# A conformer layer on 8 cores: attention outputs in any two of four PSUM banks, scaled by a stream of their own; tables loaded ahead, the gate by Tanh, the conv's square sums on TensorE

## The reference, cut to what matters

```python
x = x + 0.5 * swiglu(rmsnorm(x, ffn1_norm), ffn1_gate, ffn1_up, ffn1_down)   # inner width 2816
z = rmsnorm(x, mix_norm) @ w_in                                               # q, k, v (512 each), a, b (512 each)
attn = chunk_band_attention(q, k, v, rel_bias)                                # softmax over 576 keys
g = a * sigmoid(b)
conv = silu(layernorm(depthwise_conv(g) + dw_bias))                           # norm over the 512 channels
x = x + concat(attn, conv) @ w_out
x = x + 0.5 * swiglu(rmsnorm(x, ffn2_norm), ffn2_gate, ffn2_up, ffn2_down)
y = rmsnorm(x, final_norm)
```

## Time and profile before

| | us |
|---|---|
| three runs: median (lowest to highest) | 1470.42 (1467.99 to 1523.11) |
| the profiled execution | 1468.57 |
| its span on the slowest core, core 3 | 1467.0 |
| spans of all cores | 1463.4 to 1467.0 |
| PE / DVE / ACT / POOL busy on core 3 | 1362.0 / 493.5 / 449.2 / 275.2 |
| ACT table loads on core 3 | 43, 55.2 in all |

### The profile page before, as it was taken

How to read it: one execution, slowest core, us unless ns; L and a number is a source line. 1 busy time by engine, 2 the same in 40 slices (tenths; PEclk the granted TensorE clock), 3 DMA queues, 4 the chain that set the end, 5 groups by cost and what they waited for, 6 DMA issues and landing times.

```text
span 1467.0 us, 23437 instructions; the slowest of 8 cores (1463.4 to 1467.0 us)
## 1 busy us (share of the span) xinstructions
PE 1362.0 (93%) x8518; PEld 793.8 (54%) x8518; DVE 493.5 (34%) x854; ACT 449.2 (31%) x775; POOL 275.2 (19%) x336
## 2 busy tenths in 40 slices
PE   6899999999877999998899999997978999999996
PEld 4455555555533556564465565564635556665654
DVE  2342222254341531222552222362432562222226
ACT  2321001134276521015421011342296651101123
POOL 0117000051410300006300000340600230000013
PEclk9999999999999999999999999999989999999998
DMA  7547314524633057653357343335353034434403
GB/s 137 164 72 185 75 32 79 96 70 114 146 63 68 24 127 154 113 86 75 58 141 174 60 72 70 61 69 135 78 115 66 2 58 71 74 58 72 87 1 130
DMA packets 33738, 129.48 MB, mean 88 GB/s; under 512 B 7504, under 2 KB 12752, under 8 KB 26064
## 3 DMA queue, kind: packets, MB, share of 16 engines
q0 software_dynamic: 17856, 93.48, 34.4%
q1 hardware_dynamic: 15760, 34.41, 7.1%
HBM read 195.36 MB, written 16.55 MB: 144 GB/s over the span
## 4 chain that ended last, share of the span: by engine, by line
PE 79%; ACT 6%; DMA 5%; issue 4%; DVE 3%; POOL 3%; SPq 1%; POOLq 0%; DVEq 0%; ACTq 0%
PE psA L469 48%; PE ps L469 30%; ACT dreg L473 3%; POOL ssum L634 2%; ACT L473 2%; DMA ring<-wgu 2%; DVE hT L679 1%; DMA dreg<-gscr_1 1%; PE ps L460 1%; DMA dreg<-gscr_0 1%; DMA xres<-xin 1%; ACT rstd L473 1%; DVE xres L847 1%; DVE dreg L1244 0%; POOL ssb L639 0%
## 5 line engine op out<-in xcount | busy, mean ns | idle before, releaser
L469 PE MATMUL psA<-hT,ring 128*128 128x256 bf16 (+3 forms) x4256 | 711.5, 328 | 12.1 <-DVE hT L679 4.3
L469 PEld LDWEIGHTS psA<-hT,ring 128*128 128x128 bf16 x4256 | 410.0, 98 | 309.4 <-issue 25.6
L473 ACT ACTIVATE dreg<-psA 128x384 f32<-128x384 f32 (+6 forms) x346 | 207.0, 603 | 705.3 <-PE psA L469 699.2
L469 PE MATMUL ps<-at,ring 128*128 128x512 bf16 (+2 forms) x1936 | 328.7, 332 | 2.9 <-ACT rstd L473 2.9
L817 DVE TENSOR_TENSOR at<-psA,dreg 128x512 bf16<-128x512 f32 (+2 forms) x242 | 137.6, 569 | 487.0 <-PE psA L469 440.7
L469 PEld LDWEIGHTS ps<-at,ring 128*128 128x128 bf16 x1936 | 189.9, 98 | 138.4 <-issue 3.6
L634 POOL TENSOR_TENSOR ssum<-ssum,sq 128x256 f32<-128x256 f32 (+2 forms) x120 | 120.0, 1000 | 269.3 <-ACT sq L473 259.4
L847 DVE SCALAR_TENSOR_TENSOR xres<-ps,xres 128x512 f32<-128x512 f32 (+2 forms) x176 | 99.1, 567 | 205.7 <-PE ps L469 205.7
L562 POOL DMA_DIRECT2D ring<-wgu x45 | 24.4, 543 | 468.1 <-PE psA L469 234.9
L469 PE MATMUL ps<-dreg,ring 128*128 128x192 bf16 (+4 forms) x608 | 91.2, 310 | 15.8 <-DMA dreg<-gscr_1 8.0
L473 ACT ACTIVATE sq<-xres 128x512 bf16<-128x512 f32 (+2 forms) x126 | 65.8, 528 | 118.7 <-DVE xres L847 74.0
(11 more groups left out here) (70 smaller groups left out, 583.8 us busy)
## 6 DMA issues: line engine op xcount, KB each, us to landing
ring<-wgu POOLq DMA_DIRECT2D x43, 1024.0 KB, 9.4
ring<-wdA POOLq DMA_DIRECT2D x16, 768.0 KB, 9.6
ring<-wdB POOLq DMA_DIRECT2D x16, 640.0 KB, 7.6
ring<-cwscr POOLq DMA_DIRECT2D x16, 576.0 KB, 5.1
xres<-xin SPq DMA_DIRECT2D x10, 512.0 KB, 16.1
cwscr<-dreg SPq DMA_DIRECT2D x8, 576.0 KB, 5.1
ring<-wab POOLq DMA_DIRECT2D x8, 512.0 KB, 7.2
ring<-wout POOLq DMA_DIRECT2D x4, 1024.0 KB, 11.4
```

What stands on the lines that cost most here:

```text
L469: P.op("pe", lambda h: h.matmul(o, lhsT=lhsT, rhs=rhs, start=start, stop=stop, skip_group_check=True), max(n / 2370.0, 0.06) if dur is Non ...
L473: P.op("act", lambda h: h.activation(out=out, in_=in_, func=func, **kw), 0.19 + n / 1400.0, reads, writes)
```

## The change

- `fin1` takes whatever two banks of 4 to 7 the pair's `pv` was given (`ob`, taken from the list of free banks with its first unit). Its two products on DVE are a stream of their own at priority 0, which gives the banks back. Other users take any bank that is free, so none is reserved. A pair that would start with fewer than four banks in the list does so at priority 8.5, other attention steps at 5.
- `act` records a one-element activation of the same function ahead of one that needs another table than the last (Exp and Ln are table 0, Silu and Tanh table 1), with a planned cost of 1.5 us. It waits for nothing but a constant.
- The gate is 0.5 * (tanh(b/2) + 1) * a: Tanh with scale 0.5 on ACT, the sum and product in one DVE operation, the 0.5 in the copy into phase order.
- The square sums of the conv are 16 matmuls with `ones5`, accumulated in one bank that is held through the conv, each two channel groups after its Square. POOL keeps the plain sums.
- Silus of the conv's LayerNorm come in two steps of 8. The copy of the last 8 columns of `gp` goes to ACT.
- V and Q pieces come after conv piece 3, and conv 4 to 7 after them.

```diff
+TABLE = {AF.Exp: 0, AF.Ln: 0, AF.Silu: 1, AF.Tanh: 1}
...
-VPOS = 5
+VPOS = 4
+QPOS = 4
...
-            mode = {"fill": (4, 5, 6, 7), "lru": [4, 5, 6, 7]}
+            mode = {"lru": [4, 5, 6, 7], "table": None}
 
             def fb_best(skip=None):
-                c = [b for b in mode["lru"] if b in mode["fill"] and b != skip]
+                c = [b for b in mode["lru"] if b != skip]
...
+            def fb_two():
+                b = fb_best(fb_best())
+                return INF if b is None else P.est("pe", (), (("ps", b),))
...
             def act(out, in_, func, n, reads, writes, **kw):
+                ts = TABLE.get(func)
+                if ts is not None and ts != mode["table"]:
+                    mode["table"] = ts
+                    i = nxt("scr", 16)
+                    P.op("act", lambda h: h.activation(out=scr[0:1, i:i + 1], in_=onesS[0:1, 0:1], func=func),
+                         1.5, ("cb1",), ())
                 P.op("act", lambda h: h.activation(out=out, in_=in_, func=func, **kw),
...
-                        for i in range(8):
+                        for i in range(9):
                             if i == VPOS:
                                 addp((gi, "V"), wv_d, 4096)
-                            addp((gi, "cv", i), cw_d[i], 2304, (("cw", i),))
-                        for j in range(4):
-                            addp((gi, "Q", j), wq_d[j], 1024)
+                            if i == QPOS:
+                                for j in range(4):
+                                    addp((gi, "Q", j), wq_d[j], 1024)
+                            if i < 8:
+                                addp((gi, "cv", i), cw_d[i], 2304, (("cw", i),))
...
-                        act(tt, bb, AF.Sigmoid, n, (("ps", bB),), (("rs", ti),))
+                        act(tt, bb, AF.Tanh, n, (("ps", bB),), (("rs", ti),), scale=0.5)
...
-                        dve(lambda h, gnt=gnt, ab_=ab_, tt=tt: h.tensor_tensor(out=gnt, in0=ab_, in1=tt, op=ALU.mult), n,
+                        dve(lambda h, gnt=gnt, ab_=ab_, tt=tt: h.scalar_tensor_tensor(
+                            out=gnt, in0=tt, scalar=1.0, in1=ab_, op0=ALU.add, op1=ALU.mult), n,
...
             def conv(g):
...
+                def sq_sum(grp):
+                    k = grp % 3
+                    mm(bq, 0, ones5, sqc_t[:, k, 0:U], U, grp == 0, grp == 15, (("sqc", k), "cb1"), True)
...
+                    if bq is None:
+                        bq = fb_take()
+                        mode["lru"].remove(bq)
                     b = fb_take()
...
+                    k = grp % 3
+                    act(sqc_t[:, k, 0:U], a, AF.Square, U, (("acc", grp),), (("sqc", k),))
...
+                    if grp > 1:
+                        sq_sum(grp - 2)
...
-                    dve(lambda h: h.tensor_copy(out=gh_t, in_=gp[:, :, U:U + 8]), 128,
-                        tuple(("gp", i) for i in range(16)), ("gh",))
+                    act(gh_t, gp[:, :, U:U + 8], AF.Copy, 128, tuple(("gp", i) for i in range(16)), ("gh",))
...
                 for grp in range(16):
-                    if grp % 2 == 0:
-                        yield lambda: max(P.est("act", (("acc", grp + 1),)) - 0.2, P.t["act"] - 1.0)
+                    if grp % 8 == 0:
+                        yield lambda: max(P.est("act", (("acc", grp + 7),)) - 0.2, P.t["act"] - 1.0)
...
                     def pv(u):
                         j, pi = u["j"], u["pi"]
+                        if u["bi"] == 0:
+                            del ob[:]
+                            for e in range(2):
+                                ob.append(fb_take())
+                                mode["lru"].remove(ob[e])
+                        u["ob"] = ob
...
-                        for e in range(2):
-                            po = 64 * e
-                            o_, i0, i1 = qT[po:po + 64, j, m0:m0 + n], bank(4 + e)[po:po + 64, 0:n], rs[po:po + 64, ri, 0:n]
...
-                        F.add(("O", gi, j, s))
+                        def product(s=s, n=n, m0=m0):
+                            yield lambda: P.est("dve", (("rs", ri),)) - 0.3
...
+                            mode["lru"] += b2
+                            F.add(("O", gi, j, s))
+                        S.add(0, product())
...
-                    mode["fill"] = (6, 7)
...
-                        yield lambda: P.est("pe", (("P", u["pi"]),), (("ps", 4), ("ps", 5)) if u["bi"] == 0 else ())
+                        fn = lambda: max(P.est("pe", (("P", u["pi"]),)), fb_two() if u["bi"] == 0 else 0.0)
+
+                        fn.prio = 10 * gi + (8.5 if u["bi"] == 0 and len(mode["lru"]) < 4 else 5)
+                        yield fn
```

More of the change, by code:

```diff
@@ L422, in make @@
                 P.reg(("sq0", i), "d", O_P + 1024 * i, O_P + 1024 * (i + 1))
+            for i in range(2):
+                P.reg(("sq", i), "sq", 1024 * i, 1024 * (i + 1))
+            for i in range(3):
+                P.reg(("sqc", i), "sq", 640 * i, 640 * (i + 1))
             P.reg("asum", "d", O_AB, O_AB + 4 * UMAX)
@@ L430, in make @@
             P.reg("stage", "d", O_ACC, O_ACC + CB_N * 4)
-            mode = {"fill": (4, 5, 6, 7), "lru": [4, 5, 6, 7]}
+            mode = {"lru": [4, 5, 6, 7], "table": None}
             def fb_best(skip=None):
-                c = [b for b in mode["lru"] if b in mode["fill"] and b != skip]
+                c = [b for b in mode["lru"] if b != skip]
                 t = P.t["pe"]
+                if not c:
+                    return None
                 return min(c, key=lambda b: max(t, P.est("pe", (), (("ps", b),))))
             def fb_est():
-                return P.est("pe", (), (("ps", fb_best()),))
+                b = fb_best()
+                return INF if b is None else P.est("pe", (), (("ps", b),))
+            def fb_two():
+                b = fb_best(fb_best())
+                return INF if b is None else P.est("pe", (), (("ps", b),))
             def fb_take():
@@ L951, in glu @@
                         if P.t["act"] < P.t["dve"]:
-                            act(gd, g4, AF.Copy, n, (("gn", gi_),), (("g", gi, c),))
+                            act(gd, g4, AF.Copy, n, (("gn", gi_),), (("g", gi, c),), scale=0.5)
                         else:
-                            dve(lambda h, gd=gd, g4=g4: h.tensor_copy(out=gd, in_=g4), n, (("gn", gi_),), (("g", gi, c),))
+                            dve(lambda h, gd=gd, g4=g4: h.tensor_scalar(
+                                out=gd, in0=g4, scalar1=0.5, scalar2=None, op0=ALU.mult), n, (("gn", gi_),), (("g", gi, c),))
                         left[c] -= 1
@@ L1080, in conv @@
                         out=a, in0=bk, scalar1=bcol, scalar2=None, op0=ALU.add), U, (("ps", b),), (("acc", grp),))
[L1081 to L1094, removed]
+                    k = grp % 3
+                    act(sqc_t[:, k, 0:U], a, AF.Square, U, (("acc", grp),), (("sqc", k),))
+                    if grp > 0:
+                        wk, o_ = ("mean", mvb[:, 0, 0:U]) if grp == 15 else ("asum", sums[:, 0, 0:U])
+                        x0 = acc[:, 0, 0:U] if grp == 1 else sums[:, 0, 0:U]
+                        pool(lambda h, o_=o_, x0=x0, a=a: h.tensor_tensor(out=o_, in0=x0, in1=a, op=ALU.add), U,
+                             ("asum", ("acc", grp), ("acc", 0)), (wk,))
+                    if grp > 1:
+                        sq_sum(grp - 2)
                     if grp % 2 == 1:
@@ L1097, in conv, with conv_ln @@
                 if gi == 0:
-                    dve(lambda h: h.tensor_copy(out=gh_t, in_=gp[:, :, U:U + 8]), 128,
-                        tuple(("gp", i) for i in range(16)), ("gh",))
+                    act(gh_t, gp[:, :, U:U + 8], AF.Copy, 128, tuple(("gp", i) for i in range(16)), ("gh",))
                 F.add(("conv", gi))
-                S.add(0, conv_ln(g))
-            def conv_ln(g):
+                for grp in (14, 15):
+                    yield lambda: P.est("pe", (("sqc", grp % 3),))
+                    sq_sum(grp)
+                S.add(0, conv_ln(g, bq))
+            def conv_ln(g, bq):
                 gi, U = g.gi, g.U
                 ms, vs = mv[:, 0, 0:U], mv[:, 1, 0:U]
-                yield lambda: max(P.est("pe", ("mean", "var")), fb_est())
+                yield lambda: max(P.est("pe", ("mean",)), fb_est())
                 b1 = fb_take()
@@ L1109, in conv_ln @@
                 act(ms, bank(b1)[:, 0:U], AF.Copy, U, (("ps", b1),), ("mean",))
-                b2 = fb_take()
-                mm(b2, 0, ones5, mvb[:, 1, 0:U], U, True, True, ("var", "cb1"), True)
-                q1 = bank(b2)[:, 0:U]
+                q1 = bank(bq)[:, 0:U]
                 dve(lambda h: h.tensor_tensor(out=vs, in0=ms, in1=ms, op=ALU.mult), U, ("mean",), ("var",))
-                dve(lambda h: h.tensor_tensor(out=vs, in0=q1, in1=vs, op=ALU.subtract), U, (("ps", b2), "var"), ("var",))
+                dve(lambda h: h.tensor_tensor(out=vs, in0=q1, in1=vs, op=ALU.subtract), U, (("ps", bq), "var"), ("var",))
```

(3 more changed lines are left out.)

26 lines of the change are left out of this document (16 added, 10 removed).

## The result

The changed kernel's median is 1444.66 us, beside 1469.64 for the kernel before. The ratio is 0.9829, 95% interval 0.9807 to 0.9851: some 25 us or 1.7% less, a gain, but under 2%. The forecast was 1438 (1412 to 1464). Runs in which cores of one die show a lower clock and take longer count in the medians, which would be at most 0.9 us lower without them, but not in the ratios; the ratios of the first four experiments have wide intervals because one run of the kernel before that counts there is 1.3% longer than the rest.

A forecast was written before the change was run, and what follows sets the result against it. Limits: ACT around the conv's Silu, two-bank hand-over elsewhere in attention, PE in feed-forward. Terms saved 32.3 us odd (core 3), 26.8 even (core 2); even's 1437.1 plus 1.6 gave 1438.7, forecast 1438 us, range 1412 to 1464.

The forecast's parts named there:

- Part 2: Attention outputs in any two of four banks: 80% of filler and wait saved, 15 us odd, 16.5 even.
- ACT was the limit all along: Rival for attention: freed banks only let PE reach the next Exp sooner, giving a third; 1453 us, chance 0.20.
- a clock under 0.9 with ACT full: Sign in the attention windows that the forecast is wrong and ACT is the limit.
- Part 1: Conv Silus in two batches of 8: fewer table loads and less half clock, 14 us odd, 8 even.
- All of it through to PE: Around the conv's Silus, ACT nearly full: saved load time, 10.3 us odd and 5.1 even, all reaches PE.
- Part 3: V and Q weights earlier, tiles in the gate's wait: 2.5 us odd, 4 even; second feed-forward weights: 5 odd.
- the tiles then lack as cover in attention: V and Q tiles moved into the gate's wait: only half of 5.4 us odd and 8.2 even counts.
- the gate's wait is filled: Rival: V, Q and first pairs fill the whole wait, giving 18.7 us even instead of 4; 1424 us, chance 0.14.
- Part 4: One-element activations load tables during waits in norms and at the first gate: 3 us gained, 2 paid.
- Part 5: Conv square sums on PE cost 3.2 us odd, 3.7 even, plus 2 waiting; gate's last columns on ACT save even 3.
- one bank for everything else: Rival: during the conv, conv groups and projections between pairs share one bank and wait for evictions; 1476 us, chance 0.11.
- PE waits for ACT roughly halved: Sign that the forecast is right; before the change these waits were 26.3 us odd, 19.5 even.

The follow-up runs named there:

- the first four experiments: Changed kernel with square sums back on POOL: 0.9794; that plus two fixed banks: 0.9834; changed kernel without early activations and planned load cost: 0.9833; without activations only: 0.9828.

## Why the prediction was right, and for which wrong reasons

The total was about right (25 of some 30 us) and so was the core that ends last. The terms were not: that their errors cancel is luck, and so is core 3's end on the very value predicted.

| term | predicted, even / odd | lost when undone by itself, time | mean spans, even / odd |
|---|---|---|---|
| Silu in eights | 8 / 14 | 13.9 | 13.9 / 17.9 |
| banks (with 8 and 4 loads, see above) | 16.5 / 15 | 5.7 | 3.7 / 2.3 |
| order of the ring | 4 / 7.5 | 9.6 | 9.0 / -0.4 |
| tables early | 1 / 1 | 3.6 | 4.4 / 3.7 |
| square sums | -5.7 / -5.2 | -1.4 (not resolved) | 0.1 / -1.3 |
| Tanh | 0 / 0 | 0.6 (not resolved) | 0.4 / -0.1 |

Undone one by one they add up to 32 in the time and 31.5 in the even spans, where the change as a whole gave 25: there the parts cover for each other. On odd cores they add up to 22.1, where the change gave 27 to 29 (1463.9 to 1465.7 in the sets of the kernel before, 1436.6 after): some 5 to 7 us of the odd gain belong to no part that was undone.

- **Part 2 is the step that failed.** From a pair's cycle of 9.48 us and ACT's 6.82 in it it let 80% of filler and wait go to PE, 16.5 us even and 15 odd; undone, 5.7 showed, with more table loads in it. The filler went as said, the waits for line 1244 too, but the wait for ACT took their place. A stretch of attention of the changed kernel, core 2 (start, length):

```profile
412.74 1.21 ACT L497 ACTIVATE dreg<-ps 64x512 f32<-64x512 f32 x2
...
414.04 0.63 ACT L497 ACTIVATE dreg<-dreg 128x512 f32<-128x512 f32 x1
...
414.57 1.49 ACT L497 ACTIVATE dreg<-psA 128x1024 bf16<-128x1024 f32 x2
414.77 1.41 DVE L1287 TENSOR_TENSOR dreg<-ps,dreg 64x512 bf16<-64x512 f32 x2 [4.70 <-ACT dreg L497]
...
415.72 0.60 PE L486 MATMUL ps<-dreg,at 128*128 128x384 bf16 x4 [1.62 <-ACT dreg L497]
```

  PE's next value product waits 1.62 us for its Exp, and that stands on ACT behind two Lns and an Exp of the pair before, 1.21 + 0.63 us, without a gap. PE waits here for no bank, DVE is idle 4.70 us, and nothing of it helps. The rival *ACT was the limit all along* had this mechanism right, and the run without the second Exp shows it. Its sign, a clock under 0.9 with ACT full, did not come: in windows of 20 us from 400 to 500 and from 1070 to 1190 core 2 has a clock of 0.91 or more and ACT busy 17.5 at most, so what PE waits for are single results that come late in ACT's order, as in these lines, and not an ACT that is full. Its total of 1453 was wrong because the other parts gave more than it took over from the sum.
- **Part 1 was undersized for even**, the mechanism right: loads were counted in the order of the kernel before, 4 to be saved, where pairs in the new order need 12 more (16 on odd). "All of it through to PE" held: 15.4 us of loads, 13.9 us of time.
- **Part 3 was undersized in the second group** and had the first one wrong. 5.4 and 8.2 us of tiles were to stand in the gate's waits and half to be lost as cover. In the second group of core 2 the wait fell by 5.1, the filler around it vanished, and the clock stayed up. In the first, the loads of V and Q made the gate's trip through DRAM longer. That "the tiles then lack as cover in attention" turned out to be what decides here: *the gate's wait is filled* was made to happen twice, and cost 6.7 and 19.3 us instead of giving 14. The weights of the second feed-forward layer came as said: odd's filler from 500 to 560 us fell from 5.57 to 0.93, and the wait of 2.6 for such pieces is gone. But the 5 us taken for this did not show: in the old order core 3 has 5.13 of that filler and 1.5 of that wait again, and the odd cores end no later. Why is open.
- **Part 4**: the activation does what it says, and the 3.6 lies within its bounds of 0 to 6 less 2; that it is more than the 1 taken is not sure.
- **Part 5** was too dear, and *one bank for everything else* did not happen: the waits of PE show no eviction of a conv group above 0.2 us on core 2, and giving the held bank back changed nothing. PE did not wait behind the copy of line 1098 any more (2.9, now 0.5 for that tile's evictions). The 8.57 us of that copy look like a wait for POOL, though no run tries it alone: POOL's additions ran without a gap meanwhile, and the copy ended at 380.57 us, within 0.1 us of the last of them at 380.51 (406.00 and 405.95 on core 3). On ACT it takes 0.29.

Of the signs named, loads, line 1244, filler and the slowest core came out as said; "PE waits for ACT roughly halved" did not, and that was the sign of part 2.

## What to carry to other kernels

Before giving an accumulator more room, ask which engine the freed work queues on next: if the waits behind the buffer and those behind a busy engine take turns, as here, the gain may have to come from that engine's own instructions, and leaving one of them out for a run shows it. Work that can stand in one gap may be the cover of another; fill a gap only if the stretch that it is taken from does not wait for a different engine. Count alternations of tables in the order that the changed kernel will have, not in the old one, and count them again in every run that undoes a part: an order written by a planner changes more than the part.

## What the runs showed that was not expected

A small trip through DRAM was stretched by weight loads beside it, and the delay only shifted when the loads were held back: the gate's writes (144 KB each) took 4.7 us to land before, 9.7 with V's 1 MB issued right behind the first of them, and 2.4 with V held, when the reads took 14.4 instead of 6.3. And 27 to 35 us of idle time in front of table loads, which looked like a reserve, were worth some 3 us when they vanished: half of it (17.9 of the 34.9) was ACT waiting for PE, and 6.5 the start of the kernel.
